# Seven half products in place of a plain one in the last group of two MLPs

## The chip, the cores and the metric

The kernel runs on one core of a Trainium2 chip. The metric is the device time of one execution in microseconds (us). A core has a matrix engine (TensorE, PE in the profile; PEld is its weight load), VectorE (DVE), ScalarE (ACT), GpSimd (POOL) and SyncE (SP), which run programs of their own and wait for each other on semaphores. Matmuls write PSUM, which has eight banks of 128x512 float32 here; all else lies in SBUF.

## The reference

Two transformer layers and then a second block, on 512 tokens of width 1024, in float32. Each of the two layers ends in an MLP with squared rectifier; its hidden width is 4096.

```
def sqrelu_mlp(h, w_up, w_down):
    u = jnp.einsum('bsd,df->bsf', h, w_up)
    return jnp.einsum('bsf,fd->bsd', jnp.square(jax.nn.relu(u)), w_down)
...
x = x + sqrelu_mlp(rmsnorm(x, norm_mlp[l]), w_up[l], w_down[l])
```

Behind layer 0 come the key, value and query projections of layer 1's attention; behind layer 1 comes the second block, whose first products are the tiles g0, v0, ... of `w_in_2`.

## The kernel before, in words

**Numbers in two halves.** Every float32 operand is split in a high half (ScalarE rounds it, L1663 for weights, L1825 for activations) and a low half (VectorE subtracts, L2138 and L2140, L2374). A product is three matmuls (L999 to L1001): high by high, high by low, low by high. A slab is 1024 columns of weights for 128 rows; three buffers hold split slabs, so that a slab may be split once the slab three places before it has been used by TensorE. Slabs come by DMA into a ring of four raw buffers, or, for `w_down` in the groups below, as quarters into buffers of their own (`DB`).

**The MLP.** The hidden width is worked through in four groups of 1024, that is eight tiles U(g,0) to U(g,7) of the up projection a group (24 matmuls each). VectorE rectifies a tile (step "r", L2422), ScalarE squares it into `HF` (step "q", L1820). The down projection of a group is a product of 512 tokens by 1024 hidden by 1024 outputs. In groups 0, 1 and 2 it is made as seven half products instead of eight (Winograd's form of Strassen's scheme): the activations are quartered in A11, A12, A21, A22 (tokens by hidden), the weights likewise, and with sums S1 to S4 of activation quarters (step "S", L2368), and sums of weight quarters (step "T", L2355) seven products P(g,0) to P(g,6) of 24 matmuls do. A product takes two slabs; step "w" splits slabs up to a number, step "h" splits a product's activations. Its two bank tiles are added to the residual X (step "rd", L2391), but S2's, which belong to three places: they are gathered in `EU` over the groups (L2405) and added at the end (step "fold").

In group 3 the down projection is plain: two chunks "down" of 512 outputs, each of four slabs of 24 matmuls, 192 in all, from copies of the eight tiles that step "hc" splits (L1830, L2433).

**What sets the order.** `mlp_plan` writes one list of steps out by hand. Every engine goes through it and does its own part: P and U are TensorE's, w, h are ScalarE's and VectorE's, q ScalarE's, r, S, T, rd, fold VectorE's. So VectorE's order within a step is fixed, and what stands late in the list is late on VectorE, whatever is waiting for it. P(g,j) is interleaved with U(g+1,j); group 3's tiles stand between group 2's products.

**Behind the MLP.** In layer 0 the residual is turned for the attention by `row_turn` (TensorE L1245, ScalarE, VectorE L2455): the first half rows of tiles 0, 1 and 2 within the last chunk, tile 3 after it. A loop over the last chunk's slabs also splits two slabs ahead, the first two of the chunk "qb". Then VectorE waits for the small DMA of `b_lam`, which GpSimd issues when the last residual sum is made, works on it (L2468), sets four tiles to zero, and goes on with slabs. In layer 1 the residual is turned by `turn_first` (L1055; ScalarE L1682, VectorE L2166), squares for the norm are taken (L1669), and the slabs of g0 and v0 have been split ahead.

Of the kernel before, what the change touches and what calls it, by code (L numbers as in the profile page):

```python
# [97 lines left out]
def build(nc, cols, ins, out):  # L98
# [103 lines left out]

    ORDER = [[("A11", 4, 2, True, "11", 0), ("A12", 6, 5, True, "21", 0), ("S2", 4, 0, False, "T2", 2),
# [30 lines left out]
    for l in range(2):  # L234
# [16 lines left out]
        for g in range(3):  # L251
            for j in half_products(l, g):
# [55 lines left out]
    def t_sum(l, g, k, a):  # L308

        return S("t_sum"), 8 * (3 * l + g) + 2 * (k - 1) + a + 1  # L310

    def quarter(l, g, b, a):

        return S(f"db{b}_{a}"), 16 * (3 * l + g + 1)

    def raw_of(i):

        if i in QSLAB:
            l, g, j, a = QSLAB[i]
# [10 lines left out]
    RES = {("wo", 0): 0, ("mlp", 0): 8, ("o1", 0): 58, ("o1", 1): 62, ("o2", 0): 66, ("o2", 1): 70, ("mlp", 1): 74}  # L330
# [3 lines left out]
    def x_ready(job, t):  # L334
# [7 lines left out]
        base = {"mlp0": 4, "mix1": 54, "mlp1": 70, "pre_mix": 120}[job]  # L342
# [99 lines left out]
    def mlp_plan(l):  # L442
# [22 lines left out]
        for g in range(3):  # L465
# [20 lines left out]
            if last:
                d = CH["down", l, 0].first
                plan += [("hc", 4), ("w", d + 1), ("rd", g, 6), ("r", n, 6), ("q", n, 6), ("hc", 5), ("fold", 2, 1),
                         ("w", d + 2), ("r", n, 7), ("q", n, 7), ("hc", 6), ("w", d + 3), ("hc", 7)]
            else:  # L490
# [4 lines left out]
    PLAN_M = [mlp_plan(l) for l in range(2)]  # L495

# [216 lines left out]
    def a_of(l, j):  # L713
        hf, s3 = HFS[l], S3S[l]
        return {"A11": (hf[:, 0:4, 0:256], "h_sq", 4), "A12": (hf[:, 4:8, 0:256], "h_sq", 8),
                "S2": (hf[:, 0:4, 0:256], "hs", 3), "S1": (hf[:, 0:4, 256:512], "hs", 2), "S3": (s3[:, :, :], "hs", 1),
                "S4": (hf[:, 4:8, 0:256], "hs", 4), "A22": (hf[:, 4:8, 256:512], "h_sq", 8)}[ORDER[l][j][0]]

    def a_ready(l, g, j):
        _, name, n = a_of(l, j)  # L720
        return S(name), 8 * (4 * l + g) + n if name == "h_sq" else 4 * (3 * l + g) + n

    def h_done(l, g, j):

        return 29 * l + 7 * g + j + 1
# [120 lines left out]

    def zap(z, c):
# [27 lines left out]
    def sync_program(e):  # L875
# [3 lines left out]
        def load_quarter(l, g, b):  # L879

            j = AT[l][{"11": "S1" if l < 2 else "S2", "12": "S3", "21": "A22", "22": "S4"}[b]]
            r0, c0 = 1024 * g + 512 * (b[0] == "2"), 512 * (b[1] == "2")
            w = W["w_down"][l] if l < 2 else W["w_down_2"][0]
            if g == 0 and l < 2:
# [4 lines left out]
            for a in range(2):  # L889
                if g > 0:  # L890
                    q.wait_ge(S("w_lo"), 2 * (PS[l, g - 1, j] + a) + 2)
                    if l == 2 and b == "11":
# [3 lines left out]
                e.dma_start(DBS[l][b][a][:, :].rearrange("p (k c) -> p k c", k=2), src).then_inc(S(f"db{b}_{a}"), 16)  # L896
# [3 lines left out]
        for l in range(2):  # L900
            for m, b in ((4, "11"), (5, "12"), (6, "22"), (7, "21")):
                behind[SL["up", l, m]] = (l, 0, b)
            for g in (1, 2):
                for m, b in ((6, "11"), (7, "12"), (8, "22"), (9, "21")):
                    behind[SL["up", l, 8 * g + m]] = (l, g, b)
        for m, b in ((4, "11"), (5, "12"), (6, "21"), (7, "22")):
            behind[SL["gt", m]] = (2, 0, b)
        for x, b in ((("gt", 15), "11"), (("u2", 15), "12"), (("gt", 16), "22"), (("u2", 16), "21")):
            behind[SL[x]] = (2, 1, b)
        for i in IN_RING:  # L910
# [10 lines left out]
            if i in behind:  # L921
                load_quarter(*behind[i])
# [63 lines left out]
    def tensor_program(e):  # L986
# [193 lines left out]
        def product(l, g, j):  # L1180

            _, b, out, first, _, _ = ORDER[l][j]
            ah, al = AR[(7 * g + j) % 4]
            q.wait_ge(S("h_lo"), h_done(l, g, j))
            for a in range(2):
                _, wh, wl = next_slab()
                for t in range(2):
                    if a == 0 and out < j:
                        q.wait_ge(*out_done(l, g, out, t))
                    elif a == 0 and g > 0:  # L1190
                        q.wait_ge(*out_done(l, g - 1, out, t))
                    elif a == 0 and b == 2:

                        if l < 2:
                            q.wait_ge(S("relu"), 32 * l + 8)
                        else:
                            q.wait_ge(S("gate2"), 16)
                    for r in range(2):
                        k, x, w = 2 * a + r, slice(128 * t, 128 * t + 128), slice(512 * r, 512 * r + 512)
                        m = mm3(banks[b + t][:, :], ah[:, k, x], al[:, k, x], wh[:, w], wl[:, w], first and k == 0, k == 3,  # L1200
                                skip=True)
                m.then_inc(S("w_used"), 1)

        def mlp(l, behind=no_step):
# [12 lines left out]
            for step in PLAN_M[l]:  # L1217
# [1693 lines left out]
```

## Time and profile before

| | us |
|---|---|
| median of 3 runs (lowest, highest) | 1782.66 (1781.11, 1784.69) |
| the profiled execution's own time | 1782.82 |
| its span | 1781.0 |
| TensorE busy | 1735.4 (97%) |
| VectorE busy | 1195.6 (67%) |
| ScalarE busy | 803.4 (45%) |
| GpSimd busy | 38.1 (2%) |

The span is the time from the first to the last instruction of the program in one profiled execution. Busy time of TensorE overlaps between matmuls, so its share is no measure of how near it is to its peak; the distance from one matmul's start to the next is. The granted clock is given as a share of 2.4 GHz, and was 0.993 in the mean.

### The profile page before, as it was taken

What the parts mean: (1) busy time and instruction counts of PE and PEld (TensorE: products, weight loads), DVE (VectorE), ACT (ScalarE), POOL (GpSimd) and SP (SyncE); (2) the same over time, 40 slices, a digit from 0 to 9 for tenths busy, and PEclk for the clock granted to TensorE, in tenths of its full rate; (3) what the DMA queues carried; (4) which work ended last, traced back from release to release, by engine and by line L of the source; (5) the groups of instructions that cost most, each with busy time, mean ns of one, the idle gap of its engine ahead of it and who ended that gap; (6) DMA issues with size and microseconds to landing.
All of it is one profiled execution on the core that took longest, in us unless ns stands there. A gap on an engine that the chain in (4) does not pass through costs nothing.

```text
span 1781.0 us, 21520 instructions
## 1 busy us (share of the span) xinstructions
PE 1735.4 (97%) x8263; PEld 1425.5 (80%) x8263; DVE 1195.6 (67%) x1869; ACT 803.4 (45%) x1351; POOL 38.1 (2%) x87
## 2 busy tenths in 40 slices
PE   8999999999999999999999999999999999999998
PEld 7887888888887777777888888888787788888886
DVE  6666358687754667764777687378996544765766
ACT  7433244443434656664444344342777432333342
POOL 0000000000000021000000000000000000000000
PEclk9999999999999999999999999999999999999999
DMA  7222433333132212115242412323100353224212
GB/s 249 81 72 83 142 119 92 110 95 95 52 101 82 67 49 71 36 48 168 56 142 64 149 47 63 104 80 98 47 24 1 95 166 106 71 76 149 65 55 83
DMA packets 195750, 158.31 MB, mean 89 GB/s; under 512 B 5248, under 2 KB 161280, under 8 KB 195648
## 3 DMA queue, kind: packets, MB, share of 16 engines
q1 hardware_dynamic: 194240, 154.16, 28.6%
q0 software_dynamic: 400, 1.25, 0.3%
q8 instruction: 66, 1.08, 0.3%
q10 hardware_dynamic: 1008, 1.53, 0.2%
q14 instruction: 36, 0.29, 0.1%
HBM read 154.81 MB, written 2.10 MB: 88 GB/s over the span
## 4 chain that ended last, share of the span: by engine, by line
PE 91%; DVE 5%; ACT 3%; issue 1%; DMA 0%; POOL 0%; DVEq 0%; SPq 0%; ACTq 0%
PE ps L999 29%; PE ps L1000 28%; PE ps L1001 28%; PE ps L1464 1%; PE ps L1055 1%; ACT sb L1928 1%; PE ps L1358 0%; DVE sb L2138 0%; ACT sb L1663 0%; DVE sb L2166 0%; PE ps L1114 0%; PE ps L1329 0%; DMA sb<-in_mem 0%; PE ps L1312 0%; ACT sb L1917 0%
## 5 line engine op out<-in xcount | busy, mean ns | idle before, releaser
L999 PE MATMUL ps<-sb,sb 128*128 128x512 f32 (+5 forms) x2483 | 951.7, 390 | 8.7 <-ACT sb L1928 5.2
L1001 PE MATMUL ps<-sb,sb 128*128 128x512 f32 (+5 forms) x2483 | 931.7, 380 | 0.0
L1000 PE MATMUL ps<-sb,sb 128*128 128x512 f32 (+5 forms) x2483 | 931.6, 380 | 0.0
L2140 DVE TENSOR_TENSOR sb<-sb,sb 128x512 fp32r<-128x512 f32 (+1 forms) x418 | 391.4, 959 | 273.8 <-ACT sb L1663 273.3
L999 PEld LDWEIGHTS ps<-sb,sb 128*128 128x128 f32 (+1 forms) x2483 | 460.9, 188 | 113.4 <-issue 13.6
L1001 PEld LDWEIGHTS ps<-sb,sb 128*128 128x128 f32 (+1 forms) x2483 | 460.5, 188 | 88.9
L1663 ACT ACTIVATE sb<-sb 128x512 fp32r<-128x512 f32 (+1 forms) x418 | 338.9, 840 | 426.3 <-PE ps L1001 424.3
L1000 PEld LDWEIGHTS ps<-sb,sb 128*128 128x128 f32 (+1 forms) x2483 | 461.1, 189 | 82.7 <-issue 0.2
L1820 ACT ACTIVATE sb<-sb 128x512 f32<-128x512 f32 x64 | 40.3, 630 | 130.4 <-DVE sb L2422 130.4
L2374 DVE TENSOR_TENSOR sb<-sb,sb 128x1024 fp32r<-128x1024 f32 x56 | 68.4, 1221 | 41.8 <-ACT sb L1825 39.6
L2355 DVE TENSOR_TENSOR sb<-sb,sb 128x1024 f32<-128x1024 f32 x64 | 76.0, 1217 | 0.6
L2626 DVE SCALAR_TENSOR_TENSOR sb<-sb,sb,sb 128x512 f32<-128x512 f32 x90 | 67.4, 748 | 1.9
L2391 DVE TENSOR_TENSOR sb<-ps,sb 128x512 f32<-128x512 f32 x88 | 57.0, 682 | 4.3 <-PE ps L1001 4.0
L2422 DVE SCALAR_TENSOR_TENSOR sb<-ps,sb 128x512 f32<-128x512 f32 x64 | 43.6, 684 | 11.7 <-PE ps L1001 11.7
L2100 ACT ACTIVATE sb<-sb 128x512 f32<-128x512 f32 x22 | 13.9, 632 | 72.6 <-DVE sb L2832 72.5
L2166 DVE SCALAR_TENSOR_TENSOR sb<-ps,sb,sb 128x512 fp32r<-128x512 f32 (+1 forms) x48 | 31.0, 700 | 20.5 <-ACT sb L1682 20.5
L1825 ACT ACTIVATE sb<-sb 128x1024 fp32r<-128x1024 f32 x42 | 43.9, 1046 | 1.2 <-DVE sb L2368 1.2
L1055 PE MATMUL ps<-sb,sb 128*128 128x128 f32 x176 | 27.5, 296 | 14.8 <-DVE sb L2166 6.9
L2138 DVE SCALAR_TENSOR_TENSOR sb<-sb,sb,sb 128x512 fp32r<-128x512 f32 x40 | 29.5, 748 | 17.9 <-ACT sb L1663 17.7
L2368 DVE TENSOR_TENSOR sb<-sb 128x1024 f32<-128x1024 f32 x32 | 38.9, 1216 | 0.1
L1055 PEld LDWEIGHTS ps<-sb,sb 128*128 128x128 f32 x176 | 22.3, 151 | 20.4 <-issue 7.6
L1663 ACT ACTIVATE sb<-sb,sb 128x512 fp32r<-128x512 f32 x40 | 28.1, 715 | 10.1 <-PE ps L1001 10.1
(213 smaller groups left out, 1074.9 us busy)
## 6 DMA issues: line engine op xcount, KB each, us to landing
sb<-in_w_up SPq DMA_DIRECT2D x86, 512.0 KB, 4.1
sb<-in_w_down SPq DMA_DIRECT2D x86, 512.0 KB, 4.6
sb<-in_w_gate SPq DMA_DIRECT2D x22, 512.0 KB, 3.9
sb<-in_a_w_in SPq DMA_DIRECT2D x20, 512.0 KB, 3.8
sb<-in_w_in SPq DMA_DIRECT2D x20, 512.0 KB, 3.7
sb<-in_w_o SPq DMA_DIRECT2D x16, 512.0 KB, 3.8
sb<-in_w_mem_kv SPq DMA_DIRECT2D x8, 512.0 KB, 7.5
sb<-in_w_out SPq DMA_DIRECT2D x8, 512.0 KB, 3.8
```

What stands on the lines that cost most here:

```text
L999: mm(ps, lh, rh, start=start, stop=False, **k)
L1000: mm(ps, lh, rl, start=False, stop=False, **k)
L1001: return mm(ps, ll, rh, start=False, stop=stop, **k)
L1055: i = e.transpose(banks[4 + k % 4][:, 128 * t:128 * t + 128], src[:, t, 128 * k:128 * k + 128], IDENT)
L1663: act(WH[i % N_SPLIT][:, a], raw[:, a], ACT.Copy, scale=g).then_inc(S("w_hi"), parts)
L1825: act(AR[(7 * g + j) % 4][0], a_of(l, j)[0], ACT.Copy).then_inc(S("h_hi"), 1)
L2140: tt(lo, raw, hi, ALU.subtract).then_inc(S("w_lo"), parts)
L2355: tt(db[d][a][:, :], db[x][a][:, :], db[y][a][:, :], ALU.subtract).then_inc(S("t_sum"), 1)
L2374: tt(lo, a_of(l, j)[0], hi.bitcast(F32), ALU.subtract).then_inc(S("h_lo"), 1)
L2391: tt(x, y, x, ALU.add).then_inc(S("res"), 1)
L2422: stt(T1[:, m % 2, :], banks[u_bank(g, m)][:, :], 0.0, RB[:, :], ALU.max, ALU.mult).then_inc(S("relu"), 1)
L2626: stt(CV[:, j, :], GL[:, j, k:k + T], col("convw", 4 * k + j), CV[:, j, :], ALU.mult, ALU.add).then_inc(S("tap"), 1)
```

## The change

The last group of each of the two MLPs (`l < 2 and g == 3`) gets seven half products too, in an order and with places of its own (the fourth entry of `ORDER`). The plain chunks "down" and the steps "hc" go. P(3,0) and P(3,1) stand between U(3,6) and U(3,7), ahead of P(2,6), since A11 and S3 need only the tiles 0 to 3. Token halves are swapped in this group (`quarters_of`): A11 and A12 are tokens 256 to 511. The quarter 21 of the weights goes to the buffer `T2`; T2's sum goes to `SE`, which is made of `S3B` (free once S3 is split) and `EU` (free once the folds are made); T4's sum goes to the buffer 12. S2's product is added to X in three places directly (six sums, where `EU` took two). The last product goes token tile by token tile, both slabs each, and the early transposes of layer 0 stand between and behind the two tiles. The next chunk's first slab alone is split within the MLP (it was two). In the plan of VectorE and the others:

```diff
+    ORDER += [[("A11", 4, 2, True, "11", 0), ("S3", 6, 5, True, "12", 3), ("A12", 0, None, True, "T2", 0),
+               ("S1", 2, 6, True, "11", 1), ("S2", 4, 0, False, "SE", 2), ("A22", 6, 1, False, "12", 4),
+               ("S4", 2, 3, False, "22", 0)]]
...
+        half1, half2 = (2, 0) if kind_of(l, g) == 3 else (0, 2)
+        return {"A11": [(half1, 0)], "A12": [(half1, 0)], "S1": [(half2, 1)], "S3": [(half2, 1)], "S4": [(half1, 1)],
+                "A22": [(half2, 0)], "S2": [(half1, 1), (half2, 1), (half2, 0)] if kind_of(l, g) == 3 else []}[x]
...
-        for n in range(2):
-            CH["down", l, n] = chunk([(W["w_down"][l][3072:4096, :], 512 * n, 512)], [[2, 3], [4, 5], [6, 7], [0, 1]])
...
             if last:
-                plan += [("hc", 0), ("hc", 1), ("fold", 0, 1)]
+                plan += [("fold", 0, 1), ("fold", 2, 0)]
             plan += [("P", g, 5), ("U", n, 5), up(n, 5), ("r", n, 4), ("q", n, 4)]
...
+        plan += [("h", 3, 0), ws(3, 0, 0), ("S", 3, 3), ws(3, 0, 1), ("rd", 2, 5), ("T", 3, 1, 0), ("T", 3, 1, 1)]
+        plan += [("P", 3, 0), ("U", 3, 6), up(3, 6), ("r", 3, 5), ("q", 3, 5), ("h", 3, 1), ("T", 3, 3, 0), ws(3, 1, 0),
+                 ("T", 3, 3, 1), ws(3, 1, 1), ("rd", 3, 0), ("fold", 2, 1)]
+        plan += [("P", 3, 1), ("U", 3, 7), up(3, 7), ("r", 3, 6), ("q", 3, 6), ("T", 3, 2, 0), ("T", 3, 2, 1), ws(2, 6, 0),
+                 ("T", 3, 4, 0), ws(2, 6, 1), ("rd", 3, 1), ("T", 3, 4, 1)]
+        plan += [("P", 2, 6), ("r", 3, 7), ("q", 3, 7), ws(3, 2, 0), ("S", 3, 1), ("h", 3, 2), ws(3, 2, 1)]
+        plan += [("P", 3, 2), ("h", 3, 3), ("S", 3, 2), ws(3, 3, 0), ("rd", 2, 6), ws(3, 3, 1)]
+        plan += [("P", 3, 3), ("h", 3, 4), ws(3, 4, 0), ("rd", 3, 2), ws(3, 4, 1), ("S", 3, 4)]
+        plan += [("P", 3, 4), ("h", 3, 5), ws(3, 5, 0), ("rd", 3, 3), ws(3, 5, 1)]
+        plan += [("P", 3, 5), ("h", 3, 6), ws(3, 6, 0), ws(3, 6, 1), ("rd", 3, 4)]
+        plan += [("P", 3, 6), ("w", PS[l, 3, 6] + 3), ("rd", 3, 5), ("rd", 3, 6)]
...
+            behind[SL["up", l, 30]] = [(l, 3, "11")]
+            behind[SL["up", l, 31]] = [(l, 3, "12"), (l, 3, "21")]
+            behind[CH["qb"].first if l == 0 else SL["in", "g0"]] = [(l, 3, "22")]
...
+        def early_turns(t):
+            if t == 0:
                 row_turn(0, 0)
-            elif j == 3 and t == 3:
                 row_turn(1, 0)
+            else:
                 row_turn(2, 0)
...
-            for n in range(2):
-                c = CH["down", l, n]
-                for j in range(4):
-                    weights(c.first + j + 3)
```

## Rows read from the trace of the kernel before

**Rows 1.** The page, part 4: the chain that ended last, shares by engine
```profile
PE 91%; DVE 5%; ACT 3%; issue 1%; DMA 0%; POOL 0%; DVEq 0%; SPq 0%; ACTq 0%
```

**Rows 2.** Waits of TensorE, 230 to 560 us: in total, times, longest
```profile
PE ps L1245 <- DVE sb L2391: 1.4, 2, 1.2
```

**Rows 3.** By stretch: length, busy of PE, PEld, DVE, ACT, POOL, clock, DMA
```profile
399.00:480.00 81.00, 81.00 (x359) 67.11 (x358) 60.47 (x63) 33.12 (x38) 0.00 (x0) 1.00 0.26 78
480.00:555.00 75.00, 75.00 (x335) 62.14 (x334) 40.28 (x58) 24.32 (x39) 0.00 (x0) 1.00 0.28 88
```

**Rows 4.** Timeline of TensorE, layer 0: start, length, line, operation
```profile
549.66 0.39 PE L999 MATMUL ps<-sb,sb 128*128 128x512 f32 x1
...
554.20 0.39 PE L1001 MATMUL ps<-sb,sb 128*128 128x512 f32 x1
...
556.26 0.60 PE L1245 MATMUL ps<-sb,sb 128*128 128x128 f32 x4
```

**Rows 5.** Timelines of VectorE and ScalarE, layer 0, groups 2 and 3
```profile
455.01 0.68 DVE L2422 SCALAR_TENSOR_TENSOR sb<-ps,sb 128x512 f32<-128x512 f32 x1
457.34 1.23 DVE L2374 TENSOR_TENSOR sb<-sb,sb 128x1024 fp32r<-128x1024 f32 x1 [1.65 <-ACT sb L1825]
...
459.62 1.22 DVE L2355 TENSOR_TENSOR sb<-sb,sb 128x1024 f32<-128x1024 f32 x1
...
485.34 1.06 ACT L1663 ACTIVATE sb<-sb 128x1024 fp32r<-128x1024 f32 x1 [3.34 <-PE ps L1001]
...
487.65 0.68 DVE L2422 SCALAR_TENSOR_TENSOR sb<-ps,sb 128x512 f32<-128x512 f32 x1
```

**Rows 6.** Timelines of VectorE and TensorE, from layer 0 into layer 1
```profile
551.36 1.41 DVE L2138 SCALAR_TENSOR_TENSOR sb<-sb,sb,sb 128x512 fp32r<-128x512 f32 x2 [4.03 <-ACT sb L1663]
552.69 1.28 DVE L2391 TENSOR_TENSOR sb<-ps,sb 128x512 f32<-128x512 f32 x2
...
558.13 0.68 DVE L2391 TENSOR_TENSOR sb<-ps,sb 128x512 f32<-128x512 f32 x1
...
558.86 0.66 PE L1245 MATMUL ps<-sb,sb 128*128 128x128 f32 x4 [1.17 <-DVE sb L2391]
...
559.27 0.47 PE L999 MATMUL ps<-sb,sb 128*128 128x512 f32 x1
...
563.89 0.23 DVE L2468 TENSOR_TENSOR sb<-sb 128x64 f32<-128x64 f32 x1 [3.02 <-DMA sb<-in_b_lam]
...
564.82 0.39 PE L999 MATMUL ps<-sb,sb 128*128 128x512 f32 x1
...
565.29 1.29 DVE L2138 SCALAR_TENSOR_TENSOR sb<-sb,sb,sb 128x512 fp32r<-128x512 f32 x2
```

**Rows 7.** Timeline of all engines, from layer 1 into the second block
```profile
1155.08 1.91 PE L1055 MATMUL ps<-sb,sb 128*128 128x128 f32 x16
...
1161.30 2.40 ACT L1682 ACTIVATE sb<-ps,sb 128x512 fp32r<-128x512 f32 x4
...
1162.00 2.73 DVE L2166 SCALAR_TENSOR_TENSOR sb<-ps,sb,sb 128x512 fp32r<-128x512 f32 x4 [1.86 <-ACT sb L1682]
...
1162.85 0.46 PE L999 MATMUL ps<-sb,sb 128*128 128x512 f32 x1
...
1165.33 1.14 ACT L1663 ACTIVATE sb<-sb 128x512 fp32r<-128x512 f32 x2
```

**Rows 8.** TensorE behind three of its long waits: timeline, then by stretch
```profile
709.38 1.12 PE L1329 MATMUL ps<-sb,sb 128*128 128x128 f32 x4 [2.08 <-DVE sb L2521]
...
712.83 0.60 PE L1329 MATMUL ps<-sb,sb 128*128 128x128 f32 x4
...
709.00:713.00 4.00, 3.62 (x12) 2.96 (x13) 1.79 (x3) 0.69 (x1) 1.37 (x3) 0.57 0.43 131
...
1358.00:1362.00 4.00, 2.41 (x15) 2.17 (x16) 3.85 (x5) 3.78 (x5) 0.00 (x0) 1.00 0.00 0
...
1421.00:1424.00 3.00, 2.42 (x9) 2.05 (x10) 2.41 (x4) 2.91 (x6) 0.00 (x0) 0.50 0.59 175
```

More of the change, by code:

```diff
@@ L486, in mlp_plan @@
[L486 to L490, printed above, removed]
+                plan += [("P", g, 6), ("U", n, 6), ("U", n, 7), up(n, 6), ("r", n, 5), ("q", n, 5), up(n, 7)]
                 plan += [ws(n, 0, 0), ("rd", g, 6), ("r", n, 6), ("q", n, 6), ("T", n, 1, 0), ws(n, 0, 1), ("T", n, 1, 1),
@@ L493, in mlp_plan @@
         return plan
     PLAN_M = [mlp_plan(l) for l in range(2)]
+    OUT_RES, FOLDED = {}, {}
+    for l in range(2):
+        n = RES["mlp", l]
+        for step in PLAN_M[l]:
+            if step[0] == "fold":
+                n += 2
+                FOLDED[l] = n
+            elif step[0] == "rd":
+                g, j = step[1:]
+                each = len(goes(l, g, order(l, g)[j][0]))
+                for t in range(2):
+                    n += each
+                    OUT_RES[l, g, j, t] = n
+        assert n == RES["mlp", l] + 60
@@ L879, in load_quarter @@
         def load_quarter(l, g, b):
-            j = AT[l][{"11": "S1" if l < 2 else "S2", "12": "S3", "21": "A22", "22": "S4"}[b]]
             r0, c0 = 1024 * g + 512 * (b[0] == "2"), 512 * (b[1] == "2")
             w = W["w_down"][l] if l < 2 else W["w_down_2"][0]
+            d = "T2" if kind_of(l, g) == 3 and b == "21" else b
             if g == 0 and l < 2:
@@ L1178, in tensor_program, with product @@
         into_residual(("wo", 0), Bh, Bl, gates_ready, 0)
-        def product(l, g, j):
-            _, b, out, first, _, _ = ORDER[l][j]
+        def product(l, g, j, behind=None):
+            _, b, out, first, _, _ = order(l, g)[j]
             ah, al = AR[(7 * g + j) % 4]
             q.wait_ge(S("h_lo"), h_done(l, g, j))
[L1185 to L1202, printed above, removed]
@@ L1204, in mlp, with free @@
-        def mlp(l, behind=no_step):
+            def free(t):
+                if out is None:
+                    q.wait_ge(S("relu"), 32 * l + 31 + t)
+                elif out < j:
+                    q.wait_ge(*out_done(l, g, out, t))
+                elif g > 0:
+                    q.wait_ge(*out_done(l, g - 1, out, t))
+                elif b == 2:
+                    if l < 2:
+                        q.wait_ge(S("relu"), 32 * l + 8)
+                    else:
+                        q.wait_ge(S("gate2"), 16)
@@ new lines, in part @@
+            def part(a, t, w):
+                _, wh, wl = w
+                for r in range(2):
+                    k, x, w = 2 * a + r, slice(128 * t, 128 * t + 128), slice(512 * r, 512 * r + 512)
+                    m = mm3(banks[b + t][:, :], ah[:, k, x], al[:, k, x], wh[:, w], wl[:, w], first and k == 0, k == 3,
+                            skip=True)
+                return m
+            if behind is None:
+                for a in range(2):
+                    w = next_slab()
+                    for t in range(2):
+                        if a == 0:
+                            free(t)
+                        m = part(a, t, w)
+                    m.then_inc(S("w_used"), 1)
+                return
@@ L1205, in mlp @@
+            w = []
+            for t in range(2):
+                free(t)
+                for a in range(2):
+                    if t == 0:
+                        w.append(next_slab())
+                    m = part(a, t, w[a])
+                    if t == 1:
+                        m.then_inc(S("w_used"), 1)
+                if t == 0:
+                    m.then_inc(S("p_tile"), 1)
+                behind(t)
+        def mlp(l, behind=None):
             job = f"mlp{l}"
@@ L1292, in piece_free @@
             if c == "qb":
-                q.wait_ge(S("res"), RES["mlp", 0] + 42 + t + 1)
+                q.wait_ge(*out_done(0, 3, place_of(0, 3, "S2" if t < 2 else "A22"), t % 2))
             elif c in ("kb", "qa", "ka"):
@@ L1400, in tensor_program @@
                     piece(c, j, t, [k])
-        mlp(1)
-        q.wait_ge(S("res"), RES["mlp", 1] + 46)
+        mlp(1, no_step)
+        for t in range(2):
+            for x in ("S2", "A22"):
+                q.wait_ge(*out_done(1, 3, place_of(1, 3, x), t))
         turn_first(X, "pre_mix")
```

228 lines of the change are left out of this document (115 added, 113 removed).

## The prediction, made blind

> **What bounds the kernel now.** The chain of waits [rows 1] puts 91% of the span on TensorE. The list of TensorE's waits over the first MLP [rows 2] has one line: 1.4 us, at its end, for the last residual sums. The table by stretch [rows 3] shows why it can run so: in a group of seven half products (399 to 480) VectorE is busy 60.5 of 81.0 us, in the last, plain group (480 to 555) 40.3 of 75.0. So TensorE's matmuls are the price list as long as VectorE keeps up, and the change moves work onto VectorE where it has room on the average. The question is the order of that work.
>
> **Matmuls removed.** Between 549.66 and 554.20 stand 20 intervals [rows 4]: 4.54 / 20 = 0.227 us a matmul. The plain group has 2 x 8 x 4 x 3 = 192 of them, seven half products 7 x 24 = 168. 24 x 0.227 = 5.44 us a layer, 10.9 us in two. The up projection keeps its 24 a tile.
>
> **What VectorE gets in the last group of a layer.** Prices [rows 5]: a 128x1024 subtraction is busy 1.22 us and the next starts 1.14 us after it (457.34 to 459.62 over two; 1.135 below); a pair of 512-column sums takes 1.28 - 0.08 = 1.20 (552.69 in [rows 6]); a rectification 0.6. A rectification at 455.01 is followed by its square on ScalarE, then a first half (L1825), then the second half at 457.34: 2.33 us from start to start. A weight slab that VectorE has itself just formed costs 1.22 (the sum) + 1.05 (ScalarE's half, at 485.34) + 0.1 = 2.4 us from the sum's start to its second half's. Added: six slabs more (14 for 8), eight weight sums, four activation sums, seven second halves of 1024 for eight of 512, and 18 residual sums for 8 (S2 goes to three places). That is 6.8 + 9.1 + 4.5 + 3.1 + 6.0 = 29.5 us, on the 40.3 of [rows 3]: some 70 of 70 us. There is no room left, and the order decides.
>
> I walk the new plan with these steps in layer 0, from where both kernels are still alike. ScalarE's slab at 485.34 [rows 5] starts 0.2 after an up tile ends, so P(2,5) starts at 485.1. Check: 312 matmuls and one block of transposes (0.35) from there give 556.3, and the transposes do start at 556.26 [rows 4]. New order: P25 U35 P30 U36 P31 U37 P26 P32 ... P36. VectorE, from its rectification at 487.65 [rows 5]:
> - +2.33: second half of 3.0 at 489.98. Then two slabs, S3, two T1, U36's slab with that half are seven of 1.135, and one pair of sums: rectification 5 at 499.1.
> - +2.33: half of 3.1 at 501.5; T3a at 502.6; its slab +2.4 at 505.0; T3b at 506.1; its slab +2.4 at 508.5, done at 509.75 where TensorE wants it at 509.6: 0.2 of wait.
> - slab, two pairs of sums: U37's slab at 512.05, done 513.3 for 512.5: 0.8 of wait.
> - slab, rectification, T2a, T2b, slab, T4a, slab, pair, T4b: rectification 7 only at 521.8, though U37 ended at 518.7. Then square and ScalarE's slab: VectorE's slab at 524.2, S1, and the half of 3.2 at 526.45, done at 527.7. P26 ended at 524.2: **3.5 us of wait at P(3,2)**.
>
> In sum 4.5 us of wait a layer, 9.0 in two, against 10.9 gained. Behind P32 a product's 5.44 us hold at most 4 x 1.135 + 1.20 = 5.74 on VectorE; its tightest slab (P33) is still 0.9 early, so I take no more there. P36 starts at 549.5 and ends at 554.9: 1.0 before the old end.
>
> The Trainium skill ("VectorE: DVE Perf Modes", The DRAIN you can't avoid) says that the next operation does not start until the pipe has emptied. By it each of some 25 steps in the chain costs 0.085 more, 2 us a layer. The rows speak against it here: two 1.22 us operations start 2.28 us apart over two. I go by the rows.
>
> **Into layer 1 (only layer 0).** On VectorE, behind P36's second slab (ScalarE may begin it at half of P35, 547.0; VectorE at 548.1) stand S2's six sums, 549.25 to 552.85, then the next slab (1.33 to the next start, 551.36 to 552.69 [rows 6]), then A22's two sums, done 554.9 and 555.5. The first two early transposes need these. P36's first half is over at 552.2: **2.7 us of wait**, then 0.2 between the transposes. Second half to 558.7, last sum done at 559.6 (before: 558.13 + 0.68 = 558.81 [rows 6]). The first attention matmul comes at 559.05 for 559.27 before, with one block of transposes (0.4) still to come. The old loop also converted the attention's second slab ahead of all this; now it stands on VectorE behind row turns, the wait for b_lam and memsets. Before, b_lam ended that wait 5.08 us after the last sum (563.89), and the next slab began 1.40 later (565.29). So 559.6 + 5.08 + 1.40 + 1.41 = 567.5, where the matmuls on this slab began at 564.82 [rows 6]: **2.5 us of wait**, and 2.7 us late in all, that is 3.7 lost on the 1.0 won. Bounds of the landing: with b_lam at once, the wait is nothing (-2.5); one microsecond later, 1 more.
>
> **Into the second block (layer 1).** Turned tiles are done at about the old moment (old: 1155.08 + 1.91 [rows 7]), 0.9 lost. But v0's slab was also converted ahead, and now stands between ScalarE's squares and its turns 4 to 7 (1161.30), which VectorE (1162.00) and the matmul at 1162.85 follow directly: + 1.0, the slab's 1.14 (1165.33) less the tail. 1.9 lost; so 1.0 late.
>
> **The loads.** The group's quarters go behind up tiles 30 and 31 and the next slab, ten microseconds and more ahead of their first reader; the RAW ring gets emptier. Nothing.
>
> **The clock.** These waits are longer than most that TensorE has. After 2.08 us idle it ran at 709 to 713 with 0.57 granted, that is mostly at 1.2 GHz; at 709.38 to 712.83 [rows 8] four transposes and six matmuls take 3.45 us, and by [rows 4, 6] 0.41 + 6 x 0.227 = 1.8 at 2.4 GHz: 1.65 us lost. At 1421 to 1424, after waits of 2.0 and 2.4, it is 0.50. But 1358 to 1362, with 2.41 of 4 us busy, is 1.00. So a wait of 3.5 us costs between 0 and 1.65 more, or twice that if the low stretch is a double one; I take 1.65 for each P32 wait, being longer than those that fell, 3.3 in all, and one 1.65 for the two waits of 2.7 and 2.5 in layer 0. While the matmuls run slowly VectorE gains room, but it isn't late there, so nothing comes back. The Trainium skill ("TensorE: Matmul & The Clock Gate", What's actually happening) says that activity releases the throttle and idleness brings it back, which these rows bear out in two of three places.
>
> **Sum**, on the profiled run's 1782.8 (span 1781.0; the median of three is 1782.7, so no correction): -10.9 + 9.0 + 3.7 + 1.9 + 3.3 + 1.65 = +8.65: **1791.4 us**.
>
> **Rivals.**
> 1. The clock holds: no stretch at 1.2 GHz. All else stands: +3.7, 1786.5. For it: 1358 to 1362. Against: two places that fell after shorter waits.
> 2. VectorE keeps up: the chain is shorter than walked (a slab earlier through, TensorE's buffers bridge it), and only the passages cost, 5.6. -5.3: 1777.5. For it: the 81 us groups run without a wait with VectorE busy 75%. Against: the sum of 70 us on 70.
> 3. Only the matmuls count, passages hidden too: 1771.9. Against it stand the 1.17 us that the old passage already waits [rows 6].
> 4. VectorE doesn't recover behind P32: 5.74 against 5.44 in two products, and 0.1 to 0.2 more at each wait on its own sum, uses up the 0.9 and costs 1 to 2 us a layer more. 1794.5.
> 5. Waits as walked, but b_lam lands early and the clock holds: 1784. That is no change by what a measurement can tell, 0.2% or 3.6 us.
>
> **Chances.** Forecast 0.45 (with one low stretch fewer or more: 1788 to 1794), rival 1 0.17, rival 2 0.11, rival 3 0.03, rival 4 0.14, rival 5 0.10. Range: from between rivals 2 and 5, 1781, to a double low stretch on rival 4, 1797. Slower by over 0.2% (1786.2): forecast, rival 4, and half of rival 1: 0.68. Within: rival 5, half of 1 and a little of 2: 0.20. Faster: the rest of 2 and 3, 0.12.
>
> **What would show it.** Right: about 8215 matmul records for 8263; in TensorE's waits one of some 3.5 us at P(3,2) in each layer, ended by VectorE's second halves of activations (L2374 before), one of some 2.7 for the residual sums before the early transposes, one of 2.5 for a weight slab of the attention; granted clock below 1 right behind the first; VectorE over 95% busy from 490 to 527. Wrong: rectification 7 within 1 us of U37's end would fell the walk; a clock of 1.00 throughout would leave rival 1.

## The result, and the profile after

| | before | changed |
|---|---|---|
| median (lowest, highest), us | 1782.91 (1781.11, 1784.69), 5 runs | 1790.31 (1789.95, 1794.48), 5 runs |
| the profiled execution's own time, us | 1782.82 | 1793.71 |
| its span, us | 1781.0 | 1791.9 |
| TensorE busy, us (matmuls) | 1735.4 (8263) | 1732.5 (8215) |
| VectorE busy, us | 1195.6 | 1252.5 |

The changed kernel is slower by half a percent, a ratio of 1.0049, 95% interval [1.0034, 1.0064]. The forecast was 1791.4 in a range of 1781 to 1797.

The page of the changed kernel, first its busy time, then from part 5 the groups of weight sums, second halves of activations, residual sums and activation sums:

```profile
PE 1732.5 (97%) x8215; PEld 1419.6 (79%) x8215; DVE 1252.5 (70%) x1907; ACT 818.8 (46%) x1345; POOL 38.1 (2%) x87
...
L2449 DVE TENSOR_TENSOR sb<-sb,sb 128x1024 fp32r<-128x1024 f32 x70 | 85.5, 1221 | 48.4 <-ACT sb L1898 46.1
L2431 DVE TENSOR_TENSOR sb<-sb,sb 128x1024 f32<-128x1024 f32 x80 | 95.2, 1218 | 0.6
L2466 DVE TENSOR_TENSOR sb<-ps,sb 128x512 f32<-128x512 f32 x108 | 68.8, 682 | 1.4 <-PE ps L1054 1.4
...
L2443 DVE TENSOR_TENSOR sb<-sb 128x1024 f32<-128x1024 f32 x40 | 48.7, 1218 | 0.1
```

48 matmuls fewer, as reckoned; VectorE has 56.9 us more (28.5 a layer). What TensorE waits for is to be compared with [rows 2], where one line of 1.4 us stood. TensorE's waits in the changed kernel, layer 0 (480 to 580 us): in total, times, longest.

```profile
PE ps L1052 <- DVE sb L2449: 3.2, 1, 3.2
PE ps L1315 <- DVE sb L2466: 2.6, 1, 2.6
PE ps L1052 <- DVE sb L2207: 2.2, 1, 2.2
PE ps L1052 <- DVE sb L2209: 0.8, 2, 0.5
```

The same in layer 1 (1080 to 1180 us):

```profile
PE ps L1052 <- DVE sb L2449: 3.2, 1, 3.2
PE ps L1108 <- DVE sb L2235: 1.3, 1, 1.3
PE ps L1052 <- DVE sb L2235: 0.9, 1, 0.9
PE ps L1052 <- DVE sb L2209: 0.8, 2, 0.5
PE ps L1108 <- DVE sb L2466: 0.5, 1, 0.5
```

L2449 makes the second halves of activations (L2374 before), L2209 and L2207 those of weights, L2466 is the residual sum, L2235 the turned tile's second half, L1315 and L1108 are the transposes. So 3.2 us are lost in front of P(3,2) in each layer, 0.8 at two weight slabs, 2.6 at the early transposes, 2.2 at the attention's second slab, and in layer 1 2.8 in the passage to the second block (1.33, 0.94 and 0.49).

TensorE around P(3,2) in layer 0:

```profile
524.84 0.39 PE L1054 MATMUL ps<-sb,sb 128*128 128x512 f32 x1
528.47 0.49 PE L1052 MATMUL ps<-sb,sb 128*128 128x512 f32 x1 [3.25 <-DVE sb L2449]
...
529.33 0.63 PE L1052 MATMUL ps<-sb,sb 128*128 128x512 f32 x1
529.76 0.63 PE L1053 MATMUL ps<-sb,sb 128*128 128x512 f32 x1
...
532.68 0.39 PE L1054 MATMUL ps<-sb,sb 128*128 128x512 f32 x1
532.91 0.40 PE L1052 MATMUL ps<-sb,sb 128*128 128x512 f32 x1
```

From 524.84 to 528.47 it is 3.63 us where 0.23 is usual, so the wait costs 3.4: the list of waits counts from the end of a record of 0.39 us, while undisturbed matmuls start 0.23 apart, and a little is lost behind a wait too. Behind the wait the matmuls stand 0.43 us apart for 3.35 us (529.33 to 532.68: 1.2 GHz), then 0.23 again. Eight intervals at 0.2 us too much are 1.6 us. The granted clock by stretch says the same (columns as in [rows 3]): behind P(3,2) in layer 0, behind the attention's slab, behind P(3,2) in layer 1.

```profile
529.00:533.00 4.00, 4.00 (x12) 3.11 (x11) 4.00 (x5) 0.32 (x1) 0.00 (x0) 0.57 0.01 2
570.00:574.00 4.00, 3.94 (x12) 3.21 (x13) 1.33 (x3) 0.22 (x1) 0.12 (x1) 0.57 0.54 151
1133.00:1137.00 4.00, 4.00 (x12) 3.13 (x11) 4.00 (x4) 0.53 (x1) 0.00 (x0) 0.57 0.00 0
```

**Where the time went.** Lengths in us between starts of the same matmuls in every kernel, with the number of stretches at 1.2 GHz in each (a double one counted twice):

| from to (before's time) | before | changed | changed, again | fill, again | order | all |
|---|---|---|---|---|---|---|
| 485 to 570, group 3 of layer 0 and passage | 84.9 (0) | 91.3 (2) | 89.7 (1) | 91.3 (2) | 87.5 (2) | 80.3 (0) |
| 570 to 1090 | 520.1 (2) | 518.6 (1) | 519.0 (1) | 521.5 (3) | 518.6 (1) | 520.3 (2) |
| 1090 to 1200, the same of layer 1 | 110.0 (0) | 113.2 (1) | 113.2 (1) | 111.6 (0) | 107.9 (0) | 107.7 (0) |
| 1200 to 1460 | 259.8 (4) | 262.0 (5) | 259.9 (5) | 259.1 (3) | 260.5 (4) | 261.4 (5) |

(The last four columns are experiments, below.) In the profiled execution 6.4 us came in layer 0 and 3.2 in layer 1; of the rest of its 10.9, 0.7 came between and behind them (1.5 less, with one half-clock stretch fewer, and 2.2 more, with one more), and 0.6 at the two ends. In code that isn't changed the half-clock stretches fall in other numbers and places from kernel to kernel; one costs up to 1.6 us, less where TensorE waits within it. That goes with times of one and the same kernel that spread over 4 to 8 us. In the twelve executions of the kernel "order" below, a mean granted clock of 0.994 went with 1779.1 and 1779.4 us and one of 0.990 with 1786.5 and 1786.6.

The granted clock of every execution also says what the clock cost in the mean, and not in one profile: it was 0.9925 over 55 executions of the kernel before, which were made beside the experiments, and 0.9909 over ten of the changed kernel. The difference of 0.0016 is 2.9 us of 1790 at most (a stretch at half clock loses half its length if TensorE has work all the while), that is between one and two stretches more, not the three of this profile.

### The profile page after: what moved, and what is told of

The parts are those of the page before. It is cut to its first block and busy times, and to the rows that moved or that the text cites. A ratio compares the mean times of both kernels' runs of the same rounds, so it can differ in the third digit from the quotient of the medians.

```text
span 1791.9 us, 21502 instructions
## 1 busy us (share of the span) xinstructions
PE 1732.5 (97%) x8215; PEld 1419.6 (79%) x8215; DVE 1252.5 (70%) x1907; ACT 818.8 (46%) x1345; POOL 38.1 (2%) x87
## 3 DMA queue, kind: packets, MB, share of 16 engines
q0 software_dynamic: 400, 1.25, 0.3%
## 5 line engine op out<-in xcount | busy, mean ns | idle before, releaser
L2209 DVE TENSOR_TENSOR sb<-sb,sb 128x1024 fp32r<-128x1024 f32 (+1 forms) x414 | 405.0, 998 | 243.4 <-ACT sb L1736 242.8
L1736 ACT ACTIVATE sb<-sb 128x1024 fp32r<-128x1024 f32 (+1 forms) x414 | 349.5, 871 | 412.9 <-PE ps L1054 400.8
L2449 DVE TENSOR_TENSOR sb<-sb,sb 128x1024 fp32r<-128x1024 f32 x70 | 85.5, 1221 | 48.4 <-ACT sb L1898 46.1
L2431 DVE TENSOR_TENSOR sb<-sb,sb 128x1024 f32<-128x1024 f32 x80 | 95.2, 1218 | 0.6
L2466 DVE TENSOR_TENSOR sb<-ps,sb 128x512 f32<-128x512 f32 x108 | 68.8, 682 | 1.4 <-PE ps L1054 1.4
L1898 ACT ACTIVATE sb<-sb 128x1024 fp32r<-128x1024 f32 x56 | 58.5, 1046 | 2.5 <-DVE sb L2443 2.5
L2443 DVE TENSOR_TENSOR sb<-sb 128x1024 f32<-128x1024 f32 x40 | 48.7, 1218 | 0.1
L2235 DVE SCALAR_TENSOR_TENSOR sb<-ps,sb,sb 128x512 fp32r<-128x512 f32 (+1 forms) x48 | 31.0, 700 | 19.4 <-ACT sb L1755 19.3
L1108 PE MATMUL ps<-sb,sb 128*128 128x128 f32 x176 | 27.8, 297 | 15.7 <-DVE sb L2235 6.9
L1108 PEld LDWEIGHTS ps<-sb,sb 128*128 128x128 f32 x176 | 22.3, 152 | 21.8 <-issue 7.6
L2207 DVE SCALAR_TENSOR_TENSOR sb<-sb,sb,sb 128x512 fp32r<-128x512 f32 x40 | 29.4, 747 | 9.7 <-ACT sb L1736 9.5
L1742 ACT ACTIVATE sb<-sb 128x1024 f32<-128x1024 f32 x26 | 27.6, 1060 | 12.2 <-DVE sb L2466 4.0
```

Of the source, the lines that this page charges most:

```text
L1108: i = e.transpose(banks[4 + k % 4][:, 128 * t:128 * t + 128], src[:, t, 128 * k:128 * k + 128], IDENT)
L1736: act(WH[i % N_SPLIT][:, a], raw[:, a], ACT.Copy, scale=g).then_inc(S("w_hi"), parts)
L1898: act(AR[(7 * g + j) % 4][0], a_of(l, g, j)[0], ACT.Copy).then_inc(S("h_hi"), 1)
L2209: tt(lo, raw, hi, ALU.subtract).then_inc(S("w_lo"), parts)
L2431: tt(db[d][a][:, :], db[b][a][:, :], db[c][a][:, :], ALU.subtract).then_inc(S("t_sum"), 1)
L2443: tt(d, x, y, op).then_inc(S("hs"), 1)
```

## The experiments

Theory at the start: VectorE's work in the last group is done in an order in which the activations of P(3,2) come 3.5 us late, the passages come late for the same reason, and the idle time brings the clock down behind it. Rivals: VectorE simply has too much to do, whatever the order; or the waits are what they are but the clock costs nothing net. Each kernel is the changed one with the edit shown, and each ratio is to the kernel before.

### Short sums: the weight sums' load taken away

The eight weight sums of group 3 are made on 8 of 1024 columns, in both layers; the rest of the sums is left out.

```diff
-            tt(db[d][a][:, :], db[b][a][:, :], db[c][a][:, :], ALU.subtract)...
+            w = slice(0, 8 if x == 3 else 1024)
+            tt(db[d][a][:, w], db[b][a][:, w], db[c][a][:, w], ALU.subtract)...
```

> The kernel after, with the eight weight sums of group 3 in each MLP made on 8 of their 1024 columns: the same instructions, waits and order, but some 1.0 us less of VectorE each (this leaves out part of the computation). Theory (VectorE's load: seven of these sums stand in the chain ahead of P(3,2)): the three waits of a layer (0.25, 0.5, 3.25 us) go, and with them the stretch at 1.2 GHz behind P(3,2): 2 x (4.0 + 1.65) = 11.3 us less, 1779. Rival (it is the hand-overs between VectorE and ScalarE and the number of instructions, not their length): waits stay within 0.5 us of what they were, 1788 to 1790.

Measured 1782.88 us (1778.68 to 1786.95, 11 runs), ratio 0.9995 [0.9986, 1.0004]: 7.4 us below the changed kernel. The wait ahead of P(3,2) fell from 3.25 to 0.56 in both layers, no stretch at 1.2 GHz follows it, and the waits of 0.25 and 0.52 us went: 2 x (2.69 + 0.77) = 6.9 us of waits. The 2.6 and 2.5 us waits of the passage into layer 1 stayed, and now each had a stretch at 1.2 GHz behind it (552.1 and 565.7). The theory had 11.3 us: 1.1 of what is missing is the 0.56 left in each layer, and the profile still has 8 stretches at half clock where the changed kernel's two profiles have 9 and 8. VectorE's work is what makes P(3,2) late; whether by its amount or by its place this run doesn't tell.

### Order: the same work, moved

```diff
-... ("h", 3, 1), ("T", 3, 3, 0), ws(3, 1, 0), ("T", 3, 3, 1), ws(3, 1, 1), ...
+... ("h", 3, 1), ("T", 3, 3, 0), ("T", 3, 3, 1), ws(3, 1, 0), ws(3, 1, 1), ...
-... ("T", 3, 4, 0), ws(2, 6, 1), ("rd", 3, 1), ("T", 3, 4, 1)]
-... ("r", 3, 7), ("q", 3, 7), ws(3, 2, 0), ("S", 3, 1), ("h", 3, 2), ws(3, 2, 1)]
+... ("T", 3, 4, 0), ws(2, 6, 1)]
+... ("r", 3, 7), ("q", 3, 7), ("rd", 3, 1), ("T", 3, 4, 1), ws(3, 2, 0), ("h", 3, 2), ("S", 3, 1), ws(3, 2, 1)]
```

> The kernel after with VectorE's order changed at two places of group 3, nothing more or less to do: T3a and T3b together ahead of P(3,1)'s two slabs (2.5 us of waiting for ScalarE go), and the sums of P(3,1) and T4b behind the rectification of tile 7, where VectorE waits for the square, with the half of 3.2 ahead of S1. Theory (the order, not the load): VectorE is 2.5 us earlier at tile 7's rectification, which then waits for U37 itself, and the half of 3.2 is ready when P26 ends: all three waits and the low stretch go, 11.3 us less, 1779. Rival (the load of 70 us in 70): the wait at P(3,2) falls to 1 to 2 us or moves to P(3,3) to P(3,6): 1783 to 1787.

Measured 1782.83 us (1779.09 to 1786.57, 12 runs), ratio 0.9997 [0.9989, 1.0006], 7.5 below the changed kernel with not one instruction less. VectorE, changed kernel, from T4b to the half that P(3,2) needs:

```profile
521.38 1.22 DVE L2431 TENSOR_TENSOR sb<-sb,sb 128x1024 f32<-128x1024 f32 x1
522.52 0.68 DVE L2501 SCALAR_TENSOR_TENSOR sb<-ps,sb 128x512 f32<-128x512 f32 x1
524.92 1.23 DVE L2209 TENSOR_TENSOR sb<-sb,sb 128x1024 fp32r<-128x1024 f32 x1 [1.72 <-ACT sb L1736]
526.06 1.22 DVE L2443 TENSOR_TENSOR sb<-sb 128x1024 f32<-128x1024 f32 x1
527.20 1.22 DVE L2449 TENSOR_TENSOR sb<-sb,sb 128x1024 fp32r<-128x1024 f32 x1
```

The same place with the order changed:

```profile
517.74 0.69 DVE L2502 SCALAR_TENSOR_TENSOR sb<-ps,sb 128x512 f32<-128x512 f32 x1 [0.66 <-PE ps L1055]
518.35 1.28 DVE L2467 TENSOR_TENSOR sb<-ps,sb 128x512 f32<-128x512 f32 x2
519.54 1.22 DVE L2432 TENSOR_TENSOR sb<-sb,sb 128x1024 f32<-128x1024 f32 x1
520.68 1.22 DVE L2210 TENSOR_TENSOR sb<-sb,sb 128x1024 fp32r<-128x1024 f32 x1
521.81 1.22 DVE L2450 TENSOR_TENSOR sb<-sb,sb 128x1024 fp32r<-128x1024 f32 x1
```

The last rectification comes at 517.74 instead of 522.52, and is now what waits for TensorE. ScalarE's square and first halves then run beside the residual sums and T4b: VectorE's idle 1.72 is gone, as are two of 1.25 further up. The half is started at 521.81 instead of 527.20. The only wait left in this group is 0.72, ahead of P(3,3), for a bank that a residual sum frees late. So the load as it is doesn't force the 3.2 us: with every sum still made, another order is enough to take the wait away. The theory's 1779 wasn't reached. The rival had the wait move to P(3,3), which it did with 0.72 of it in each layer, and both waits of layer 0's passage now had a stretch at half clock behind them (551.9 and 565.6), where the changed kernel's profile had one.

### Pairs: the first of the two moves alone

```diff
-... ("h", 3, 1), ("T", 3, 3, 0), ws(3, 1, 0), ("T", 3, 3, 1), ws(3, 1, 1), ...
+... ("h", 3, 1), ("T", 3, 3, 0), ("T", 3, 3, 1), ws(3, 1, 0), ws(3, 1, 1), ...
```

> The kernel after with only the first of the two reorderings: T3a and T3b together, then P(3,1)'s two slabs. Theory: waits of 0.25 and 0.5 go, the one at P(3,2) falls from 3.25 by 2.5 less these 0.75, to 1.5: 5 us less in two layers, and the low stretches too if 1.5 us is too short for them: 1782 to 1785.3. Rival (VectorE isn't what P(3,2) waits for in the end): only 1.5 us less, 1788.8.

Measured 1787.2 us (1782.29 to 1787.83, 11 runs), ratio 1.0015 [1.0006, 1.0024]. This is 3.1 below the changed kernel and nearer to the rival's 1788.8 than to the theory's range. The two waits of 0.25 and 0.52 are gone, and so are VectorE's two of 1.25: a sum of weights followed by the halves of that same sum leaves VectorE idle while ScalarE makes the first half. VectorE reaches the half of P(3,2) 2.47 us earlier (524.73 for 527.20), as the theory had it. The wait ahead of P(3,2) is 2.1 in both layers, 1.1 less, where a fall of 1.7 was expected: the two small waits had cost more than their gaps say. From start to start they were 0.5 and 0.8 us, 1.3 for 0.77, and 1.3 + 1.1 = 2.4. Half-clock stretches still fell behind both waits (526.1, 1126.8).

### Fill: TensorE kept busy through the wait, run twice

Twelve matmuls into a bank that is free, ahead of P(3,2), in both layers; nothing reads them.

```diff
+            if l < 2 and (g, j) == (3, 2):
+                q.wait_ge(S("relu"), 32 * l + 31)
+                for _ in range(12):
+                    mm(banks[0][:, :], Ah[:, 0, 0:128], Ah[:, 1, :], start=True, stop=True)
             q.wait_ge(S("h_lo"), h_done(l, g, j))
```

> The kernel after, with twelve more matmuls (128x512, into a bank that P(3,2) starts anew) in TensorE's wait ahead of P(3,2), in both layers: 2.7 us of work that nobody needs in a wait of 3.25. Theory (the idle time lowers the clock, 1.65 us lost each): no low stretch behind P(3,2), 3.3 us less although TensorE does more: 1787. Rival (the low stretch would come anyway, or costs nothing since VectorE sets the pace): 1790, or more where the fillers run over the wait's end.

Measured 1792.32 us (1789.32 to 1794.54, 5 runs), ratio 1.0046 [1.0033, 1.0058]. Its profiled execution was 4.4 below that of the changed kernel, its median 2.0 above, where the rival had put it. As the two disagree, it was run once more, beside the changed kernel on one chip:

> Twelve matmuls into a bank that is free fill the wait ahead of P(3,2) in both layers, beside the changed kernel on the same chip. Clock theory: the wait itself stays, but the stretches at 1.2 GHz behind it go, 1.65 each: 1786.5 to 1788.5, that is 1.6 to 3.3 less than the changed kernel beside it. Rival (the stretches only move to later waits of 2 us and more, so that their number over the whole kernel is what it was): 1789.5 to 1792.5, within 1 of the changed kernel.

> The changed kernel itself once more, as the yardstick for the one beside it on the same chip. Expected: 1790 (1789 to 1794.5), with waits of 3.2 us ahead of P(3,2) and half-rate stretches behind at least one of them. If the spread inside the kernel is that of stretches at 1.2 GHz falling or not falling elsewhere, its times lie in steps of about 1.65 us.

Measured: fill 1793.24 us (1787.59 to 1795.96, 6 runs), ratio 1.0048 [1.0034, 1.0062]; changed kernel 1791.4 us (1789.36 to 1794.22, 5 runs), ratio 1.0046 [1.0033, 1.0059]. TensorE at P(3,2) with the fill:

```profile
525.01 2.88 PE L1240 MATMUL ps<-sb 128*128 128x512 f32 x12
528.42 0.50 PE L1052 MATMUL ps<-sb,sb 128*128 128x512 f32 x1 [0.52 <-DVE sb L2453]
528.76 0.40 PE L1053 MATMUL ps<-sb,sb 128*128 128x512 f32 x1
529.00 0.40 PE L1054 MATMUL ps<-sb,sb 128*128 128x512 f32 x1
529.23 0.40 PE L1052 MATMUL ps<-sb,sb 128*128 128x512 f32 x1
```

The fill does its work on the spot: the clock stays up behind P(3,2) in both layers, and the section of layer 1 is 1.6 us shorter for it (111.6 for 113.2). But in the second run both later waits of layer 0 then had a stretch behind them (557.1 and 570.8), and 570 to 1090 had three for one. In its two profiled executions the fill had 7 and 8 stretches over the whole kernel (tail aside), the changed kernel 9 and 8. The rival expectation is the right one in that the number of stretches over the whole kernel isn't lower: over its eleven executions the fill's mean granted clock is 0.9905, the changed kernel's over ten is 0.9909. Two stretches fewer would have raised it by 0.002. (The median, 1.8 above the changed kernel's, lies just over the rival's range too; with executions from 1787.6 to 1796.0 that is no difference.) The two intervals for the fill and the two for the changed kernel leave no room for a gain of the full 3.3 us; one of 1 us can't be told from none. Why the stretches shift so is open.

### Slab first: the attention's second slab ahead of the wait for b_lam

```diff
         row_turn(3)
+        weights(CH["qb"].first + 2)
         q.wait_ge(S("lam_in"), 48)
```

> The kernel after, with VectorE's half of the attention's second slab made ahead of the wait for b_lam instead of behind it. Theory: TensorE's wait of 2.2 us for that slab goes, and in the profiled pattern the low stretch behind it (1.65): 2.2 to 3.9 us less, 1786.5 to 1788. Rival (VectorE is late there anyway, and the wait moves to the next slab or to the row turns): less than 1 us, 1789.5 or more.

Measured 1790.89 us (1789.08 to 1792.01, 5 runs), ratio 1.0039 [1.0027, 1.0052]. The wait of 2.2 is gone from the list, and the section of layer 0 is 2.8 shorter (88.4, with two half-clock stretches as in the changed kernel: the one that had followed the removed wait now follows the 2.6 us wait, at 557.1). The profiled execution is 2.8 below the changed kernel's, but the median lies between that kernel's two medians (1790.31 and, in a later set of runs, 1791.4): a gain of 2.2 to 2.8 isn't seen in the total, nor excluded by the interval. The granted clock shows where it may have gone: 0.9892 in the mean of these five executions (0.991 in the profiled one, 0.988 or 0.989 in the others) for 0.9909 in the changed kernel, up to 3.0 us. Why the clock was lower isn't shown.

### GpSimd: four of the eight sums a layer on the idle engine

T2's and T4's sums are made by GpSimd instead of VectorE.

```diff
+        def sums_3(l):
+            ...
+            for a in range(2):
+                q.wait_ge(*quarter(l, 3, "22", a))
+                TTT(db["SE"][a][:, :], db["22"][a][:, :], db["11"][a][:, :], ALU.subtract)...
+            for a in range(2):
+                ...
+                TTT(db["12"][a][:, :], db["T2"][a][:, :], db["SE"][a][:, :], ALU.subtract)...
```

> The kernel after, with the four sums T2 and T4 of group 3 made by GpSimd, which is idle there. Theory: four of 1.135 us leave VectorE's chain ahead of P(3,2), the wait of 3.25 and the stretch at 1.2 GHz go, those of 0.25 and 0.5 stay: 2 x 4.9 = 9.8 us less, 1780.5. Rival (GpSimd's work slows VectorE's two-input subtractions, or a sum takes it over 5 us, so that P(3,4) or P(3,5) waits): 1786 or more, with VectorE's subtractions longer than 1.22 us while GpSimd works.

Measured 1798.54 us (1797.8 to 1799.56, 5 runs), ratio 1.0083 [1.007, 1.0095]: 8.2 slower than the changed kernel. GpSimd's four sums in layer 0, one by one:

```profile
513.04 3.16 POOL L992 TENSOR_TENSOR sb<-sb,sb 128x1024 f32<-128x1024 f32 x1 [512.60 <-DVE sb L2483]
516.16 2.39 POOL L992 TENSOR_TENSOR sb<-sb,sb 128x1024 f32<-128x1024 f32 x1
518.52 3.38 POOL L997 TENSOR_TENSOR sb<-sb,sb 128x1024 f32<-128x1024 f32 x1
521.86 3.38 POOL L997 TENSOR_TENSOR sb<-sb,sb 128x1024 f32<-128x1024 f32 x1
```

VectorE at the same time:

```profile
512.72 1.22 DVE L2226 TENSOR_TENSOR sb<-sb,sb 128x1024 fp32r<-128x1024 f32 x1
513.85 0.69 DVE L2518 SCALAR_TENSOR_TENSOR sb<-ps,sb 128x512 f32<-128x512 f32 x1
516.26 3.38 DVE L2226 TENSOR_TENSOR sb<-sb,sb 128x1024 fp32r<-128x1024 f32 x1 [1.72 <-ACT sb L1753]
519.56 3.42 DVE L2226 TENSOR_TENSOR sb<-sb,sb 128x1024 fp32r<-128x1024 f32 x1
522.90 1.28 DVE L2483 TENSOR_TENSOR sb<-ps,sb 128x512 f32<-128x512 f32 x2
```

The Trainium skill ("SBUF — State Buffer", SBUF: two separate sides) says that a VectorE operation with two SBUF inputs and a GpSimd operation that reads SBUF lock each other out for whole instructions. The trace agrees: the two take turns. GpSimd's second sum, which began before VectorE's first subtraction, takes 2.39 us and ends at 518.55; VectorE's subtraction, begun at 516.26, ends 1.09 later, at 519.64, and is recorded as 3.38 for 1.22. GpSimd's next sum ends 2.26 after that, at 521.90, VectorE's next 1.08 after that. So the 3.38 of each are mostly waiting.

From 516.26 to 522.90 the two second halves of weights take 6.6 us where two such subtractions take 2.3 in the changed kernel: 4.4 lost. VectorE is rid of four sums, 4.5 us, but 1.7 of these it now waits for ScalarE, whose work the sums used to cover. That makes it 1.6 us later, and the half of 3.2 is started at 528.77 instead of 527.20. The wait ahead of P(3,2) grew to 4.0 in both layers. The rest of the 8.2 us is in good part the clock: 0.9886 in the mean of the five executions for 0.9909, up to 4.1 us.

### Passages: the two passages alone, the wait at P(3,2) left as it is

The slab first as above, S2's six sums ahead of the second slab of P(3,6), A22's two sums ahead of the next chunk's slab, and v0's slab split within layer 1's plan again.

```diff
-... ("h", 3, 6), ws(3, 6, 0), ws(3, 6, 1), ("rd", 3, 4)]
-        plan += [("P", 3, 6), ("w", PS[l, 3, 6] + 3), ("rd", 3, 5), ("rd", 3, 6)]
+... ("h", 3, 6), ws(3, 6, 0), ("rd", 3, 4), ws(3, 6, 1)]
+        plan += [("P", 3, 6), ("rd", 3, 5), ("w", PS[l, 3, 6] + 3), ("rd", 3, 6)]
+        if l == 1:
+            plan += [("w", PS[l, 3, 6] + 4)]
```

> The kernel after, with the passages alone changed: the attention's second slab ahead of the wait for b_lam; S2's six sums ahead of P(3,6)'s second slab and A22's two sums ahead of the next chunk's slab; v0's slab within the second MLP. Theory: the waits of 2.6 and 2.2 us behind layer 0 and the low stretch there go (6.4), layer 1's passage gains 1.0, and P(3,6)'s second slab costs at most 0.5: about 7 us less, 1783.5. Rival (the sums set the passage whatever the order, since VectorE has the same work): the 2.2 alone, 1788.

Measured 1785.64 us (1782.85 to 1788.58, 11 runs), ratio 1.0014 [1.0005, 1.0022]. In layer 0 the waits of 2.6 and 2.2 are gone and the section is 6.3 shorter (85.0, one half-clock stretch for two): what the prediction gave to this passage, and more. In layer 1 only 0.9 was won: the wait for the turned tiles is 1.9 in place of 1.3 + 0.9. That v0's slab was the cause of 1.0 there is thus at best half right; taking it away left most of the wait. The total is 4.7 below the changed kernel, between the theory's 7 (1783.5) and the rival's 2.2 (1788).

### All: order and passages together

The edits of "order" and of "passages", both.

> Both reorderings and the passages together. Theory (independent terms): 11.3 and 7 us less than the kernel after, 1772, that is 11 under the kernel before, which is the price of the 48 matmuls. Rival (VectorE's load is left over and shows as soon as the order doesn't): 1777 to 1781.

Measured **1777.47 us (1775.52 to 1778.36, 5 runs), ratio 0.9965 [0.9954, 0.9977]**: faster than the kernel before, by 5.9 us against the before runs beside it (1783.32), and 12.8 below the changed kernel, by the same instructions in another order. TensorE's waits in layer 0:

```profile
PE ps L1055 <- DVE sb L2212: 1.0, 1, 1.0
PE ps L1055 <- DVE sb L2469: 0.7, 1, 0.7
PE ps L1151 <- DVE sb L2266: 0.6, 1, 0.6
```

And in layer 1:

```profile
PE ps L1111 <- DVE sb L2238: 1.9, 1, 1.9
PE ps L1055 <- DVE sb L2212: 1.0, 1, 1.0
PE ps L1055 <- DVE sb L2469: 0.7, 1, 0.7
```

From 518 to 550 us, by stretch, columns as in [rows 3]:

```profile
518.00:550.00 32.00, 30.27 (x134) 24.20 (x133) 32.00 (x37) 17.05 (x19) 0.00 (x0) 1.00 0.00 1
```

VectorE is busy for all 32 us, and the waits of 1.0 and 0.7 in this stretch are those of an engine that has no room. Here the load is the bound, as the rival said (1777 to 1781), and that is 3.4 of the 5.5 us by which it isn't the 1772 of the theory; whether still another order would do better isn't shown. Layer 1 loses more: its section is 2.3 below the kernel before, layer 0's 4.6, of 5.4 each, and its 1.9 us wait for the turned tiles isn't explained. Of the 10.9 us that the matmuls free, half is kept.

## Why the prediction was right

- **Matmuls removed, -10.9.** 48 records fewer, as said. The interval of 0.227 us stands (544.73 to 554.48 in the changed kernel: 43 intervals in 9.75 us). The price itself no run took apart.
- **VectorE's added work.** 29.5 us a layer were reckoned, 28.5 measured. The reading beside it was wrong: "There is no room left" and over 95% busy from 490 to 527. VectorE was busy for 30.61 of these 37 us, 83%. The other 6.4 us are waits for ScalarE's first halves (the last 0.5 of one, then 1.65, 1.25, 1.25 and 1.72), which were in the walk's steps (2.33 and 2.4 us) but not in the sum of loads. The walk was right, the summary was not; the run with the changed order shows the difference.
- **The walk to P(3,2), 4.5 a layer.** The changed kernel runs 0.55 us later from the start of the program. Less that, the walk against the trace: rectification 5 at 499.1 (499.14), second half of 3.1 at 501.5 (501.47), rectification 7 at 521.8 (521.97), the half of 3.2 at 526.45 (526.65). As gaps the waits are 3.25, 0.25 and 0.52 for 3.5, 0.2 and 0.8. What the walk counts is the delay from start to start, and that is more: from P(2,5)'s first matmul (485.62) to P(3,2)'s (528.47) it is 42.85 us, of which 168 matmuls at 0.227 are 38.14. The delay is 4.7 for 4.5. The steps from start to start, 1.135 us, carried 25 operations to within 0.2 us; the alternative that was weighed, 0.085 more for each, would have been 2 us off.
- **Passage into layer 1, +3.7.** 2.64 us of wait at the early transposes for 2.7, 2.17 at the slab for 2.5. From the last residual sum's end (561.55 + 0.69) to b_lam's operation (567.33) it is 5.09 us for 5.08, and 1.39 to the next slab for 1.40. Taking the two causes away took away the two waits: the causes are shown, and their sum is right within 0.4 us.
- **Passage into the second block, +1.9.** 2.8 us of wait in the changed kernel, 1.3 of it as before. With the order changed and no half-clock stretch, the section of layer 1 is 2.1 us shorter than before (107.9 for 110.0); its 5.4 us of matmuls less 0.7 of wait left in the group give 4.7, so the passage costs 2.6. The sum was 0.7 too small, and its cause, v0's slab alone, isn't borne out.
- **The clock, +4.95.** Forecast were three stretches more than before, 1.65 each. In the profiled execution there were three more (nine for six), and at just the places named: behind P(3,2) in both layers and in layer 0's passage. The cost of one is 1.6, read from the intervals. But this execution is the second longest of its five (1793.71 us for a median of 1790.31), the second profile had two more, and the mean granted clock of ten executions gives 2.9 us at most. The term was too large by 2 us or more. Its attribution failed too: the fill took the stretches away from P(3,2), and neither the total fell nor the mean granted clock rose. That the waits at P(3,2) cost the term isn't shown.
- **The sum.** +8.65 was forecast. The two sections gave 9.6 (6.06 and 2.6 were forecast for them, 6.4 and 3.2 came), the profiled execution was 10.9 above before and the median 7.4. The difference between these last two is about two half-clock stretches. Without the clock the sum was +3.7; the two sections less their three stretches of 1.6 give 4.8, since the walk cost 0.2 a layer more and the passage into the second block 0.7 more. So the waits were a little too small and the clock too large, and that the median came out within 1.1 us of the forecast is in part luck. The path, the order on VectorE and the waits it makes, is what was right.

Rival 4, VectorE not recovering behind P(3,2), is refuted for the changed kernel: between that wait and the early transposes no other stands. Rivals 2 and 3 fell with the waits, and rival 5 with b_lam. Rival 1, 1786.5 with the clock up throughout, was 3.8 below the median.

## What to carry to other kernels

Added work on an engine that is 67% busy isn't hidden by its free share: walk its program through, start to start, with each wait for another engine's half as a step, and see when it reaches the operation that the bound engine waits for. Then change the order before taking the change back: independent work belongs between a step and the one that needs another engine's answer to it, and what a bound engine's next product needs goes ahead of what a later one needs. Here the same instructions made 1790 us in one order and 1777 in another.

## What the runs showed of the hardware

- A 128x1024 float32 sum of two SBUF inputs takes GpSimd 2.39 us when it starts first. Beside VectorE's subtractions of two SBUF inputs the two engines take turns, and each operation is recorded as 3.38 to 3.42 us, for 2.39 and 1.22. Moving four sums a layer off VectorE made the kernel 8.2 us slower.
- A wait of 2.1 to 3.25 us ahead of matmuls is sometimes followed by a stretch at 1.2 GHz (3.4 us long, 1.6 us lost) and sometimes not, in the same kernel and place: the 2.17 us wait at the attention's second slab had one behind it in the first profile of the changed kernel (570.1) and none in the second. The 3.25 us wait ahead of P(3,2) had one in both layers of both profiles, but not in layer 1 of the run "passages". Filling it with twelve matmuls kept the clock up in four of four places, and the mean granted clock of the whole execution stayed as low as before (0.9905 and 0.9909).
- A wait costs TensorE more than the gap in the list of waits: 0.5, 0.8 and 3.4 us from start to start for gaps of 0.25, 0.52 and 3.25.
